# A convolution branch's layer norm in a two-block float32 layer: the mean summed in the attention's tail, the variance summed token by token, and parked gates loaded by SyncE's queue

## What is computed

```python
a, ag = jnp.split(conv_in, 2, axis=-1)
u = a * jax.nn.sigmoid(ag)
u = ... depthwise causal convolution of u, 31 taps, 512 channels ... + conv_b
u = jax.nn.silu(layer_norm(u, conv_ln_g, conv_ln_b))
br_conv = u @ w_conv_out
...
p_m = jax.nn.softmax(s_m, axis=-1)                 # attention over 256 memory rows
br_mem = o_m @ w_mem_out
gm = jax.nn.sigmoid(g_merge).reshape(b, s, N_BRANCH, D_MODEL)
merged = gm[:, :, 0] * br_nsa + gm[:, :, 1] * br_conv + gm[:, :, 2] * br_mem
h = x + merged @ w_out
```

## Time and profile before

| | us |
|---|---|
| median of 3 runs | 1909.08 (1906.58 to 1912.51) |
| profiled execution, its own time | 1905.19 |
| profiled execution, span | 1903.6 |
| TensorE busy | 1835.0 (96%) |
| ScalarE busy | 584.8 (31%) |
| VectorE busy | 832.6 (44%) |
| GpSimd busy | 765.5 (40%) |
| mean granted clock | 0.974 |

### The profile page before, as it was taken

How to read it: one execution, slowest core, us unless ns; L and a number is a source line. 1 busy time by engine, 2 the same in 40 slices (tenths; PEclk the granted TensorE clock), 3 DMA queues, 4 the chain that set the end, 5 groups by cost and what they waited for, 6 DMA issues and landing times.

```text
span 1903.6 us, 23507 instructions
## 1 busy us (share of the span) xinstructions
PE 1835.0 (96%) x8837; PEld 1361.5 (72%) x8837; DVE 832.6 (44%) x1263; ACT 584.8 (31%) x1082; POOL 765.5 (40%) x629
## 2 busy tenths in 40 slices
PE   9999979999999999999899889999999999999999
PEld 6888757775887444443688776777778878888887
DVE  4121665455443233232523576999338552202221
ACT  3223334443232111110231334555435222212221
POOL 4444423333540000000232548888825544544452
PEclk9999989999998999999899899999999999999999
DMA  6323212223333899999422322222253323233321
GB/s 224 99 79 99 78 55 84 84 84 139 106 127 137 317 352 392 338 371 374 149 88 91 125 96 95 67 67 73 71 207 111 122 77 100 91 98 100 94 95 44
DMA packets 81895, 266.36 MB, mean 140 GB/s; under 512 B 8320, under 2 KB 9344, under 8 KB 81792
## 3 DMA queue, kind: packets, MB, share of 16 engines
q1 hardware_dynamic: 61152, 224.02, 33.8%
q10 hardware_dynamic: 18336, 32.51, 4.7%
q0 software_dynamic: 2304, 8.39, 1.3%
HBM read 248.11 MB, written 16.78 MB: 139 GB/s over the span
## 4 chain that ended last, share of the span: by engine, by line
PE 89%; DVE 6%; ACT 2%; DMA 1%; issue 1%; ACTq 1%; POOL 0%; SPq 0%; POOLq 0%; DVEq 0%
PE psum L560 86%; DVE root L1888 1%; PE psum L900 1%; PE psum L1238 1%; ACTq L1794 1%; DVE area L1904 1%; DMA more<-stream 1%; PE psum L674 1%; DVE area L2430 1%; DVE area L1963 1%; PE psum L868 0%; ACT area L1385 0%; ACT root L1385 0%; DVE yt_lo L2211 0%; ACT ring_hi L1385 0%
## 5 line engine op out<-in xcount | busy, mean ns | idle before, releaser
L560 PE MATMUL psum<-area_r,ring_hi 128*128 128x512 f32 (+1 forms) x3168 | 995.1, 396 | 8.8 <-DVE area_r L1857 2.4
L458 POOL TENSOR_TENSOR ring_lo<-ring,ring_hi 128x512 fp32r<-128x512 f32 x436 | 584.9, 1364 | 898.8 <-ACT ring_hi L1385 893.8
L560 PEld LDWEIGHTS psum<-area_r,ring_hi 128*128 128x128 f32 x3168 | 591.6, 190 | 146.8 <-issue 21.4
L560 PE MATMUL psum<-area_r,ring_lo 128*128 128x512 f32 (+1 forms) x1584 | 617.7, 390 | 0.0
L1385 ACT ACTIVATE ring_hi<-ring 128x1024 fp32r<-128x1024 f32 x218 | 229.8, 1057 | 610.9 <-PE psum L560 559.9
L560 PEld LDWEIGHTS psum<-area_r,ring_lo 128*128 128x128 f32 x1584 | 300.2, 190 | 62.4
L1385 ACT ACTIVATE area<-psum 128x512 f32<-128x512 f32 (+3 forms) x256 | 124.2, 512 | 210.0 <-PE psum L674 71.4
L1888 DVE RECIPROCAL root<-root 128x512 f32<-128x512 f32 (+1 forms) x30 | 94.1, 3137 | 134.3 <-ACT root L1385 134.3
L560 PE MATMUL psum<-area 128*64 128x128 f32 (+6 forms) x832 | 112.1, 346 | 14.6 <-DVE area L1889 9.7
L560 PE MATMUL psum<-ring,area 128*64 128x512 f32 (+1 forms) x416 | 108.9, 619 | 0.2 <-issue 0.2
L560 PE MATMUL psum<-more,area 128*64 128x512 f32 x384 | 92.6, 604 | 8.9 <-DVE area L2206 6.7
(11 more groups left out here) (219 smaller groups left out, 1660.0 us busy)
## 6 DMA issues: line engine op xcount, KB each, us to landing
ring<-stream SPq DMA_DIRECT2D x324, 512.0 KB, 3.5
more<-stream SPq DMA_DIRECT2D x48, 1024.0 KB, 7.2
area<-gates ACTq DMA_DIRECT2D x40, 256.0 KB, 5.8
gates<-root ACTq DMA_DIRECT2D x24, 256.0 KB, 2.0
gates<-area ACTq DMA_DIRECT2D x16, 256.0 KB, 2.8
area<-xT SPq DMA_DIRECT2D x8, 256.0 KB, 4.5
area<-xT ACTq DMA_DIRECT2D x8, 256.0 KB, 3.6
tokens<-area ACTq DMA_DIRECT2D x2, 1024.0 KB, 4.2
```

Of the source, the lines that this page charges most:

```text
L458: ins = nc.gpsimd.tensor_tensor(ring_lo[:, c % RS, n], ring[:, c % R, n], ring_hi[:, c % RS, n].bitcast(F32), ALU.subtract)
L560: return nc.tensor.matmul(out, lhsT, rhs, start=first, stop=last)
```

## The change

1. The mean's sum is put into the attention's tail: `attention` gets an argument `tail`, called once after the last scores, and the sum goes to bank 3 instead of bank 6. It waits for the last exponential of the scores (`me`) instead of the last output copy (`mov`).
2. The variance is summed token by token: for each of the four squared tiles, four matmuls with 128 tokens of the tile as the stationary operand and one column of ones as the moving one, into 4 columns of bank 7. They stand between `branch(0, 0)` and `branch(0, 1)`. The root and the reciprocal are taken over 128x4. Four matmuls with an identity matrix then spread the result over bank 6, behind `branch(0, 1)`, and VectorE multiplies from there.
3. The 36 unread matmuls are gone. `branch(0, 4)` waits for the split tiles one at a time.
4. The 24 loads of the gates move from ScalarE's queue to SyncE's, between the loads of the stream's chunks `merge2 + 8` and `merge2 + 9`.
5. ScalarE touches the square root and the silu once on one element ahead of their use (`preload`), which brings the load of their tables forward.

```diff
@@ SyncE
-            segment(CMP1 + R, NCHUNK, w_lo, R - 1 + MOE1 - MOE0 + CMP1 - CMP0)
+            MERGE = C0["merge2"] + 9
+            segment(CMP1 + R, MERGE, w_lo, R - 1 + MOE1 - MOE0 + CMP1 - CMP0)
+            sp.wait_ge(weights_used, C0["gate2"] + 3 * KD)
+            for j in range(2):
+                sp.wait_ge(S(f"gate_kept{j}"), 16 * 5 * KD // 2)
+            def gates2(p, js):
+                for m in (2 * p, 2 * p + 1):
+                    for j in js:
+                        sp.dma_start(tile(GATES2[j][m]), gates_dram[2 * KD + 3 * m + j]).then_inc(S(f"gates_in{p}"), 16)
+            gates2(0, (0, 1))
+            sp.wait_ge(S("mo"), 16)
+            sp.wait_ge(S("conv_out"), 2 * TAPS)
+            sp.wait_ge(S("conv_pool"), 2 * TAPS)
+            gates2(0, (2,))
+            for p in range(1, 4):
+                gates2(p, (0, 1, 2))
+            segment(MERGE, NCHUNK, w_lo, R - 1 + MOE1 - MOE0 + CMP1 - CMP0)
@@ TensorE, attention()
                 for u in range(len(units) + 3):
+                    if u == len(units) and tail is not None:
+                        tail()
@@ TensorE, after it
-            pe.wait_ge(S("gate_raw"), 5 * KD)
-            pe.wait_ge(S("mov"), 4)
-            pe.wait_ge(S("conv_out"), 2 * TAPS)
-            pe.wait_ge(S("conv_pool"), 2 * TAPS)
-            for c in range(CONVT):
-                ins = mm(psum[:, 6, :], ones[:], tile(CV + c), c == 0, c == CONVT - 1)
-            ins.then_inc(S("ln_sum"), 1)
+            def conv_sum():
+                pe.wait_ge(S("me"), 16)
+                pe.wait_ge(S("conv_out"), 2 * TAPS)
+                pe.wait_ge(S("conv_pool"), 2 * TAPS)
+                for c in range(CONVT):
+                    ins = mm(psum[:, 3, :], ones[:], tile(CV + c), c == 0, c == CONVT - 1)
+                ins.then_inc(S("ln_sum"), 1)
...
+                if n == 3:
+                    pe.wait_ge(S("ln_d"), CONVT)
+                def split_tile(k):
+                    if br == "cv" and n == 4:
+                        pe.wait_ge(S("br_split"), 9 + k)
+                    return tr(src[0][k]), tr(src[1][k])
...
             pe.wait_ge(S("br_split"), 4)
             branch(0, 0)
-            branch(0, 1)
-            wide(16, 5)
+            pe.wait_ge(S("gate_raw"), 5 * KD)
             for c in range(CONVT):
                 pe.wait_ge(S("ln_sq"), c + 1)
-                ins = mm(psum[:, 7, :], ones[:], tile(SCR2 + c), c == 0, c == CONVT - 1)
+                for t in range(NT):
+                    ins = mm(psum[:, 7, t:t + 1], tile(SCR2 + c)[:, P * t:P * t + P], ones[:, 0:1], c == 0 and t == 0,
+                             c == CONVT - 1 and t == NT - 1)
+            ins.then_inc(S("ln_sum"), 1)
+            branch(0, 1)
+            pe.wait_ge(S("ln_root"), 2)
+            pe.wait_ge(S("mov"), 4)
+            for t in range(NT):
+                ins = mm(psum[:, 6, P * t:P * t + P], root[:, 1, t:t + 1].to_broadcast([P, P]), ident[:], True, True)
             ins.then_inc(S("ln_sum"), 1)
             pe.wait_ge(S("br_split"), 8)
-            branch(0, 2)
-            branch(0, 3)
-            wide(20, 5)
-            pe.wait_ge(S("br_split"), 12)
-            branch(0, 4)
-            branch(0, 5)
+            for e in range(2, 6):
+                branch(0, e)
@@ ScalarE
             act.wait_ge(S("mt"), 16)
-            act.wait_ge(S("conv_out"), 2 * TAPS)
-            act.wait_ge(S("conv_pool"), 2 * TAPS)
-            for j in range(2):
-                act.wait_ge(S(f"gate_kept{j}"), 16 * 5 * KD // 2)
-            for m in range(KD):
-                for j in range(3):
-                    n = 3 * m + j
-                    act.dma_start(tile(GATES2[j][m]), gates_dram[2 * KD + n]).then_inc(S(f"gates_in{m // 2}"), 16)
             for c in range(CONVT):
                 act.wait_ge(S("ln_d"), c + 1)
                 A(tile(SCR2 + c), tile(CV + c), ACT.Square).then_inc(S("ln_sq"), 1)
+            preload(ACT.Sqrt, 6)
+            act.wait_ge(S("gate_kept1"), 16 * 5 * KD // 2)
             act.wait_ge(S("ln_sum"), 2)
-            A(root[:, 0, :], psum[:, 7, :], ACT.Sqrt, eps[:, 1:2], 1.0 / (CONVT * P)).then_inc(S("ln_root"), 1)
+            A(root[:, 1, 0:NT], psum[:, 7, 0:NT], ACT.Sqrt, eps[:, 1:2], 1.0 / (CONVT * P)).then_inc(S("ln_root"), 1)
+            preload(ACT.Silu, 7)
@@ VectorE
-                V.scalar_tensor_tensor(out=tile(CV + c), in0=psum[:, 6, :], scalar=-1.0 / (CONVT * P), in1=tile(CV + c),
+                V.scalar_tensor_tensor(out=tile(CV + c), in0=psum[:, 3, :], scalar=-1.0 / (CONVT * P), in1=tile(CV + c),
...
-            link(V.reciprocal(root[:, 0, :], root[:, 0, :]))
+            V.reciprocal(root[:, 1, 0:NT], root[:, 1, 0:NT]).then_inc(S("ln_root"), 1)
+            dve.wait_ge(S("ln_sum"), 3)
             dve.wait_ge(S("ln_sq"), CONVT)
             for c in range(CONVT):
-                V.tensor_tensor(tile(CV + c), tile(CV + c), root[:, 0, :], ALU.mult).then_inc(S("ln_n"), 1)
+                V.tensor_tensor(tile(CV + c), tile(CV + c), psum[:, 6, :], ALU.mult).then_inc(S("ln_n"), 1)
```

More of the change, by code:

```diff
@@ L641, in normed, with attention @@
                             S("hdsum"), 1)
-            def attention(kind, fill=None):
+            def attention(kind, fill=None, tail=None):
                 units, maps = score_items(kind)
@@ L1274, in _ @@
             pe.wait_ge(S("nov"), 4)
-            attention("mem", fill=lambda u: gate2(4 * NT + u // 2, (0, 1, 2, 3) if u % 2 == 0 else (4, 5, 6, 7)))
-            pe.wait_ge(S("gate_raw"), 5 * KD)
-            pe.wait_ge(S("mov"), 4)
-            pe.wait_ge(S("conv_out"), 2 * TAPS)
-            pe.wait_ge(S("conv_pool"), 2 * TAPS)
-            for c in range(CONVT):
-                ins = mm(psum[:, 6, :], ones[:], tile(CV + c), c == 0, c == CONVT - 1)
-            ins.then_inc(S("ln_sum"), 1)
+            def conv_sum():
[5 more added lines that the diff above has]
+                ins.then_inc(S("ln_sum"), 1)
+            attention("mem", fill=lambda u: gate2(4 * NT + u // 2, (0, 1, 2, 3) if u % 2 == 0 else (4, 5, 6, 7)),
+                      tail=conv_sum)
             def branch(p, e):
@@ L1293, in branch @@
                        "cv": ([CVH + x for x in range(4)], [CV + x for x in range(4)])}[br]
-                ins = by_tile(c, n % 8, lambda k: (tr(src[0][k]), tr(src[1][k])), off=off, nk=4, used=False)
+                if n == 3:
[4 more added lines that the diff above has]
+                    return tr(src[0][k]), tr(src[1][k])
+                ins = by_tile(c, n % 8, split_tile, off=off, nk=4, used=False)
                 if merge_freed(p, m, br):
```

## The result

| | before | changed |
|---|---|---|
| median of the runs | 1910.11 us (4 runs) | **1896.57 us** (4 runs, 1894.63 to 1898.36) |
| ratio | 1 | 0.9931, interval 0.9914 to 0.9949 |
| profiled execution, span | 1903.6 us | 1893.0 us |

The change is faster by 13.5 us in the medians, between 9.7 and 16.4 us by the interval.

The account below looks back on a forecast made before the run. ScalarE's issuing of gate loads ahead of the squares was taken to bound the stretch. TensorE's path of 21.88 against 31.41 us gains 9.5, less 1.6 for the clock: 7.9, so 1897.3 profiled, 1901.2 median, range 1897.0 to 1904.8.

Parts of the forecast that it names:

- The chain that set the time before: Up to 1433.20 us: ScalarE's 24 gate loads (12.78 us) ahead of the squares, then variance sum, root, reciprocal, multiplications, splits.
- The sum of 21.88 us: TensorE's rebuilt path from 1401.79 us to the first convolution piece, against 31.41 before: 9.5 us gain without waits.
- the 0.45 us charged each time pieces follow plain float32 matmuls: Surcharge on TensorE's pieces: two behind a full-width sum took 5.89 us, 0.45 more than 5.44.
- The tail: Rest of the attention's tail on TensorE: 2.85 us before, 2.25 expected, with 0.6 of its 0.77 us wait gone.
- The narrow matmuls at 3.49: Variance in 16 one-column float32 matmuls: 3.49 us, as in the first norm, 0.35 slower than the full-width sum.
- the spreading at 0.81: Four matmuls spreading the narrow result behind the second piece: 0.81 us, read at the norm ahead of the feed-forward part.
- The clock: Near the narrow matmuls: brief fall costs 1.6 us (chance 0.50); stays up 0.27; long fall costs 4.8 us (0.10).
- a sign of being wrong: A clock at full level throughout; the forecast expected 0.50 for about 3 us near the second piece.
- What the narrow variance buys: Root and reciprocal over 128x4 take 0.87 us, covered by the second piece; the full reciprocal's 3.35 us leave the chain.
- The loads on SyncE: Cost nothing in the sum; issue delays stream chunk `merge2 + 9` by some 13 us, to about 1420.
- a new hole: Rival at the convolution piece: slowed splits or late squares make TensorE wait; gain 3.5 us or less, 1905.6; chance 0.09.
- a slower kernel: Rival: stream chunk `merge2 + 9` lands over 10 us late behind the gates; 16 late gives 1915.6 us; chance 0.04.

## Why the prediction was right or wrong

- *The chain that set the time before*: right. After the change TensorE has no wait up to the next norm, and all of the difference between the two profiles sits in the stretch.
- *What carries the gain*: right, that it takes the moved loads and the new order together, and now shown from both sides. The loads alone give nothing (130.57 us), the unread matmuls alone lose 5.0, both together give 1.16, and the new order without the moved loads loses 5.8 against before. Within the new order the mean's sum in the tail is worth 1.76 us at full clock and the narrow variance nothing. The earlier place of the variance's sum and the wait for each split tile were not tested apart.
- *The sum of 21.88 us*: it came out at 20.99. **The step that failed is the 0.45 us charged each time pieces follow plain float32 matmuls.** It was read at one place, behind a full-width sum, and charged at three where no such sum stands directly ahead. Behind the attention's values a piece took 2.85, behind the narrow matmuls 2.86, and two behind the spreading 5.56, not 3.17, 3.17 and 5.89: 0.12 to 0.14 us more than the bare pieces, not 0.45. The other 0.33 go with full-width sums alone, and the mean's sum pays them in its new place: 3.43 instead of 3.10. The tail took 1.99 instead of 2.25, most of it because the whole wait of 0.77 went. The narrow matmuls at 3.49 and the spreading at 0.81 were exact. With 20.99 in the sum the same range would have begun at 1896.1 and held the median.
- *The clock*: the size was right (120.67 against 119.12), the chance was about right. It fell in three of the six profiles in which 16 narrow matmuls stand between full work. The forecast time rested on a fall; the first profile had none, which the prediction had named as a sign of being wrong. These two, 0.9 and 1.6 us, are nearly all of the 2.7 us by which the profiled execution lies below its forecast (1894.63 against 1897.3), and 2.5 of the 4.6 us between forecast and median. What the clock did in the runs without a profile isn't known.
- *The rest*, some 2 us, is another term: the forecast put the median 3.9 us above the profiled execution, as before, and it came out 1.94 above. That is scatter, as far as these runs tell, and so the last 0.43 us below the range are in part bad luck: the two later timings lie inside it. The same kernel was timed at 1896.57, 1898.38 and 1897.72, with ratios 0.9931, 0.9936 and 0.9954; the trace's 10.6 us are a ratio of 0.9944, inside every one of the three intervals. That nothing outside the stretch gives time is shown for the first pair of profiles only. A range from 1897.0 left too little for the scatter of a median of four. Its own terms reach from 1897.9 to 1903.3 (1899.6 - 0.2 - 1.5 and 1901.2 + 0.6 + 1.5), not from 1897.5 to 1903.5.
- *What the narrow variance buys*: wrong. I read a reciprocal of 3.35 us on the chain before and took it for a cost to be removed. In the new order, with a wait per tile, it is hidden but for 1.1 us, and the narrow form costs 1.11 us of TensorE and adds the clock's risk.
- *The rule on the clock* that I weighed, from the Trainium skill, page "TensorE: Matmul & The Clock Gate", section "HAM oscillation — how this bites in real kernels", lays the lower clock to TensorE's waits. The waits of 10.69 and 4.18 us agree with it. The falls behind narrow matmuls, where TensorE had none, don't.
- *The loads on SyncE*: right. The next stream load went out at 1421.03, one microsecond from the estimate, and TensorE waited for nothing up to the next norm. The rivals of a new hole and of a slower kernel did not come.

## What to carry to other kernels

Rebuild the busiest engine's path from its own rows and then test every join: a price of changing over that is read at one place holds for that pair of neighbours only. A long operation on a chain costs time only in an order that leaves nothing to run beside it, so try the order and finer waits before the cheaper operation. Instructions that only issue transfers belong on a queue that no one waits for, and that pays only together with the order that uses it.

## What the hardware showed that I had not expected

- Sixteen float32 matmuls of one column, 3.5 us without a pause, were followed by three microseconds at 1.2 GHz in three of six profiles of nearly the same code, at a price of 1.55 us. In the program's first norm the same run was followed by the lower clock in ten of fourteen profiles. Within a run of 32 it fell in all fifteen places seen. The unread full-width runs of the kernel before, 3.8 and 4.7 us without a pause, had none.
- At half clock a chain of sums on TensorE is hit in full: 6.96 us for the narrow sums, 6.09 for the full-width one.
- A second semaphore ahead of an activation moved its table's load of 1.28 us behind the wait; one element touched ahead of the waits keeps the load in front of them.
